# Decoder layer on one core: first norms of blocks 1 to 3 turned before weight and bias, branch products read a row sooner, five value sums on TensorE, projection products placed by load

## The chip, the core and the metric

One core of a Trainium2 chip runs the whole program. The metric is device microseconds of that core. Its engines are TensorE (PE; its weight loads are PEld), VectorE (DVE), ScalarE (ACT), GpSimd (POOL) and SyncE (SP); transfers run on 16 DMA engines. Each engine takes its own instructions in program order and waits on semaphores for the others.

## What is computed

One decoder layer on 512 tokens of width 1024, in f32:

```
z      = x @ W_in                      9 sections of 1024: q, forget, input, out-gate, B, C, h, gate_a, gate_b
o_A    = gated linear recurrence (8 heads) of the first four sections
o_B    = B * causal_depthwise_conv3(C * h)
mix    = (sigmoid(gate_a) * (o_A @ W_a) + sigmoid(gate_b) * (o_B @ W_b)) @ W_out
x      = LayerNorm(alpha * x + mix)
x      = LayerNorm(alpha * x + PEER(x))
x      = x + sigmoid(x @ W_pg) * (p @ W_pp)
```

PEER: queries x @ w_q of 8 heads, two halves each, are scored against 128 keys a half; the 16 best pairs of a head name 16 of 16384 experts. Of each, a row of 2048 numbers (u, then v) is gathered per token, and the output is the sum of softmax weight x gelu(u . x) x v.

## The kernel before

**Rows.** Tokens come in four blocks of 128. A "row" is one of 512 gathers: for 128 tokens, the expert of one head and one rank, 128 x 2048 numbers, 1 MiB. Block b has rows 128b to 128b + 127, 16 for each head. Each engine has a loop over all rows, with fixed work at fixed rows. For row r:

- GpSimd issues the gather into a ring of buffers (`uv`, L726): six, a seventh for rows 98 to 127, more from row 212 on. `row_previous(r)` is the row that had the buffer, `v_reader` the semaphore of the engine that took its v sum; GpSimd waits for that. From row 99 to row 132 it is seven rows back.
- VectorE makes the product u . x (`dot`, L1607).
- ScalarE makes gelu and the coefficient (`row`, L985, L989).
- The v sum, coefficient x v, is taken either by VectorE (rows in `SHARED`; `sum_v` at L1620 into `acc`, one row later) or by TensorE (the others; L2122, two products of 128x512 with a diagonal matrix that ScalarE makes at L997).

In block 0 all rows up to 102 are SHARED, then every third from 109 to 121.

**What else runs under block 0.** The mixer and the first norm of block 0 are done before row 0. For blocks 1 to 3 together (384 tokens) they are spread over the rows of block 0, by tables of rows computed at the top of `build`:

- `UNITS`, rows 0 to 62: 38 of 40 products of 1024 x 128 columns of W_in (h, C, B, then the two gates), eight `unit_mm` each (L2022), in four PSUM banks. The tables name the row `UNIT_ROW` of each product on TensorE; ScalarE (`unit_out`) and VectorE (`conv_in`, `conv_tap`, `conv_out`) read a unit 1 to 4 rows after `UNIT_END`. TensorE doesn't wait for a row as such, only for weights and for the bank's reader four units back. Queries of block 0, heads 4 to 7, stand at rows 0, 4, 14 and 24 (`QUERY0_ROW`).
- `MERGE_ROW`, rows 63 to 86: 16 branch products with W_a and W_b (L2041); VectorE multiplies each with its gate (`merge`, L1373) and adds the two branches (L1378) three rows after its end, the last at row 89.
- `OUT_ROW`, rows 88 to 99: 12 output chunks (L2055), each behind the last merge; VectorE adds the residual three rows later (L1386).
- `NORM_ROW` 95, 99, 103: VectorE's `norm1_stats` (L1393); a row later aggregate and `norm1_scale`: (x - mean) x weight (L1400); two rows later `norm1_shift`: x reciprocal root + bias (L1410), which counts `x1_done`. ScalarE's `root_of` (L978) stands one row after NORM_ROW.
- `TURN_ROW` 98, 102, 106: TensorE transposes the normed block (`turn_x`, L2069), ScalarE copies it out a row later (`turn_out`, L936). SyncE waits for x1_done = 4 before it loads the 4 MiB of `w_gate` (L672) over the place of the first norm's weight and bias; the query weights of heads 2 and on are fetched behind it.
- `QUERY_ROW`, from row 108: queries and scores of blocks 1 to 3; search for the experts of block 1's first heads.

On TensorE, up to row 99 (`JOBS_FIRST`) the tail work of row r comes first and then the v sum of row r - 1; from there the v sum of row r comes first. At row 126 TensorE adds `acc` (`add_acc`), at rows 124 and 129 it makes the second norm's weight and bias rows (`ln2_row`).

## Time and profile before

| | before |
|---|---|
| median of 3 runs | 1788.03 us (1782.82 to 1788.03) |
| profiled execution | 1787.28 us |
| its span, first to last instruction | 1785.3 us |
| busy: PE, DVE, ACT, POOL | 88%, 74%, 44%, 28% |
| gathers | 536.9 of 654.4 MB, 72.9% of the 16 DMA engines' time |
| first gather issued | 336.06 us |

Of the page's 40 slices (44.6 us each) two lines tell most; the first 14 show the mixer of block 0, units and branch products, slices 15 to 19 the stretch of output chunks, norms and first queries and the change from block 0 to block 1:

```profile
DMA  5113289999999999999999999999999999999994
GB/s 210 66 67 141 98 323 397 353 417 409 415 416 416 416 395 356 411 377 413 402 422 410 417 421 422 421 420 422 421 421 422 421 415 422 421 421 419 421 422 180
```

A digit is the busy share in tenths; a rate of about 420 GB/s is what the core reaches in undisturbed slices. In a window's row, the column behind PEclk (granted clock of TensorE as a share of full speed) is the DMA engines' share, then their rate; a share over 1 comes from packets that overlap. In a timeline, idle time before an instruction stands in brackets, with the instruction that ended it. Rows are counted from 0 by L1607's instructions on VectorE (the one at 342.78 us is row 0) and by L726's on GpSimd.

### The profile page before, as it was taken

What the parts mean: (1) busy time and instruction counts of PE and PEld (TensorE: products, weight loads), DVE (VectorE), ACT (ScalarE), POOL (GpSimd) and SP (SyncE); (2) the same over time, 40 slices, a digit from 0 to 9 for tenths busy, and PEclk for the clock granted to TensorE, in tenths of its full rate; (3) what the DMA queues carried; (4) which work ended last, traced back from release to release, by engine and by line L of the source; (5) the groups of instructions that cost most, each with busy time, mean ns of one, the idle gap of its engine ahead of it and who ended that gap; (6) DMA issues with size and microseconds to landing.
All of it is one profiled execution on the core that took longest, in us unless ns stands there. A gap on an engine that the chain in (4) does not pass through costs nothing. (4 is left out here: it accounts for less than half of the span.)

```text
span 1785.3 us, 16920 instructions
## 1 busy us (share of the span) xinstructions
PE 1572.3 (88%) x5008; PEld 876.8 (49%) x5008; DVE 1322.0 (74%) x2717; ACT 780.5 (44%) x1936; POOL 497.0 (28%) x528
## 2 busy tenths in 40 slices
PE   9999999999999978999888668888889879788778
PEld 7888888766555546454344222333333323232224
DVE  4454588699988999578877876876666677766676
ACT  6666695422222124354343434434444443444453
POOL 0000000122332222323333433433333333333341
PEclk9999999999999988999899989999999999999999
DMA  5113289999999999999999999999999999999994
GB/s 210 66 67 141 98 323 397 353 417 409 415 416 416 416 395 356 411 377 413 402 422 410 417 421 422 421 420 422 421 421 422 421 415 422 421 421 419 421 422 180
DMA packets 104501, 654.35 MB, mean 367 GB/s; under 512 B 10336, under 2 KB 25440, under 8 KB 28128
## 3 DMA queue, kind: packets, MB, share of 16 engines
q0 software_dynamic: 73728, 536.90, 72.9%
q1 hardware_dynamic: 30400, 115.92, 17.0%
q8 instruction: 37, 0.61, 0.1%
q10 hardware_dynamic: 288, 0.52, 0.1%
q14 instruction: 48, 0.39, 0.1%
HBM read 651.21 MB, written 2.10 MB: 366 GB/s over the span
## 5 line engine op out<-in xcount | busy, mean ns | idle before, releaser
L2122 PE MATMUL psum<-uv,diag 128*128 128x512 f32 x1400 | 699.8, 631 | 184.2 <-ACT diag L997 180.7
L1607 DVE CUSTOM_DVE_ANT_0 uv<-uv,psum 128x1024 f32<-128x1024 f32 x512 | 623.0, 1217 | 298.3 <-DMA uv<-in_pk_uv,idx 291.8
L726 POOL DMA_INDIRECT uv<-in_pk_uv,idx x512 | 494.6, 966 | 1253.3 <-PE psum L2122 560.3
L2122 PEld LDWEIGHTS psum<-uv,diag 128*128 128x128 f32 x1400 | 254.8, 196 | 600.5 <-ACT diag L997 380.4
L985 ACT ACTIVATE gelu<-dots 128x1 f32<-128x1 f32 x512 | 103.5, 202 | 755.5 <-DVE dots L1607 753.2
L1620 DVE SCALAR_TENSOR_TENSOR oT<-uv,coef,oT 128x1024 f32<-128x1024 f32 x157 | 201.0, 1281 | 1.5 <-ACT coef L989 1.5
L989 ACT ACTIVATE coef<-gelu,weight 128x1 f32<-128x1 f32 x512 | 150.9, 295 | 16.6
L997 ACT ACTIVATE diag<-ident,coef 128x128 f32<-128x128 f32 x350 | 140.6, 402 | 11.5
L2022 PE MATMUL psum<-xT,raw 128*128 128x384 f32 x384 | 125.8, 486 | 0.0
L1858 PE MATMUL psum<-xTh,w_hi 128*128 128x512 f32 x248 | 98.6, 398 | 0.0
L1858 PE MATMUL psum<-xTl,w_hi 128*128 128x512 f32 x248 | 96.8, 390 | 0.0
L1858 PE MATMUL psum<-xTh,w_lo 128*128 128x512 f32 x248 | 96.5, 389 | 0.0
L2022 PEld LDWEIGHTS psum<-xT,raw 128*128 128x128 f32 x384 | 72.4, 190 | 48.8
L2089 PE MATMUL psum<-oT,raw 128*128 128x384 f32 x256 | 92.2, 492 | 0.0
L1133 DVE TENSOR_TENSOR w_lo<-raw_a,w_hi 128x1024 fp32r<-128x1024 f32 x32 | 39.2, 1225 | 69.4 <-ACT w_hi L741 69.1
L2089 PEld LDWEIGHTS psum<-oT,raw 128*128 128x128 f32 x256 | 49.5, 194 | 46.1 <-issue 25.7
L1858 PEld LDWEIGHTS psum<-xTl,w_hi 128*128 128x128 f32 x248 | 46.5, 188 | 10.1
L1858 PEld LDWEIGHTS psum<-xTh,w_lo 128*128 128x128 f32 x248 | 46.6, 188 | 9.1
L1858 PEld LDWEIGHTS psum<-xTh,w_hi 128*128 128x128 f32 x248 | 46.6, 188 | 8.9
L741 ACT ACTIVATE w_hi<-raw_a 128x1024 fp32r<-128x1024 f32 x32 | 34.0, 1062 | 31.4 <-PE psum L1858 27.9
L2185 PE MATMUL psum<-w_gate,x2T 128*128 128x512 f32 x96 | 47.6, 592 | 0.0
L985 ACT ACT_TABLE_LOAD x36 | 46.2, 1283 | 0.6
(295 smaller groups left out, 1856.6 us busy)
## 6 DMA issues: line engine op xcount, KB each, us to landing
raw<-in_w_in SPq DMA_DIRECT2D x24, 1024.0 KB, 8.7
raw_a<-in_w_a SPq DMA_DIRECT2D x12, 1024.0 KB, 4.7
raw<-in_pk_w_q SPq DMA_DIRECT2D x10, 1024.0 KB, 9.1
raw_y<-in_w_in SPq DMA_DIRECT2D x8, 1024.0 KB, 6.8
uv<-in_pk_uv,idx POOLq DMA_INDIRECT x512, 14.7
raw<-in_w_branch_a SPq DMA_DIRECT2D x6, 1024.0 KB, 7.2
raw_w<-in_pk_w_q SPq DMA_DIRECT2D x6, 1024.0 KB, 9.1
raw<-in_w_out SPq DMA_DIRECT2D x5, 1024.0 KB, 14.9
```

Of the source, the lines that this page charges most:

```text
L726: pool.indirect_dma_start(row_uv(r)[:], None, pk_uv, bass.IndirectOffsetOnAxis(idx[:, i % 2, j:j + 1], 0)).then_inc(row_loaded(r)[0], 16)
L985: nc.scalar.activation(gelu[:, r % 4:r % 4 + 1], dots[:, r % 32:r % 32 + 1], ACT.Gelu).then_inc(gelu_done, 1)
L989: nc.scalar.activation(coef[:, r % 8:r % 8 + 1], gelu[:, r % 4:r % 4 + 1], ACT.Copy, scale=weight[:, i % 2, j:j + 1]).then_inc(coef_done, 1)
L997: nc.scalar.activation(diag[:, n % DR, :], ident[:], ACT.Copy, scale=coef[:, r % 8:r % 8 + 1]).then_inc(diag_done, 1)
L1133: V.tensor_tensor(w_lo[:, s], raw_a[:, slot, half], w_hi[:, s].bitcast(F32), ALU.subtract).then_inc(lo_done, 1)
L1607: V.tensor_tensor_reduce(u, u, x_cur[:], 1.0, 0.0, ALU.mult, ALU.add, dots[:, r % 32:r % 32 + 1]).then_inc(dot_done, 1)
L1620: V.scalar_tensor_tensor(out=acc, in0=v, scalar=c, in1=acc, op0=ALU.mult, op1=ALU.add).then_inc(acc_step, 1)
L1858: last = T.matmul(B[bk][:], w[:, s, k, :], xx[:, k, :], start=(k == 0 and i == 0), stop=(k == KT - 1 and i == 2))
L2022: last = T.matmul(B[bank(r)][:, 0:SEQ - P], slot(SLOT["unit", n // 2])[:, k, half * P:half * P + P], xT[:, k, P:], start=(k == 0), stop=(k ...
L2089: last = T.matmul(B[bank(r)][:, 0:n], w[:, k, a * P:a * P + P], turned[:, k, :], start=(k == 0), stop=(k == KT - 1), skip_group_check=True)
L2122: last = T.matmul(B[i][:], diag[:, n % DR, :], row_uv(r)[:, D + i * 512:D + (i + 1) * 512], start=(r in FIRST), stop=last_of_block, skip_g ...
L2185: last = T.matmul(B[6 + i][:], x2T[:, k, :], w_gate[:, k, i * 512:(i + 1) * 512], start=(k == 0), stop=(k == KT - 1), skip_group_check=True)
```

## The change

- Units get their rows from a table of costs (a product 0.654, a query 4.3) so that rows with a query get none or few.
- SHARED leaves out rows 90, 93, 96, 99 and 102: their v sums go to TensorE.
- Merges of the last eight branch products come one row after their end instead of three.
- Norms of blocks 1 to 3: in NORM_ROW statistics and aggregate; the root in the same row; in the next row (x - mean) x reciprocal root (`normed`), which counts x1n_done; TURN_ROW one row earlier. ScalarE puts weight and bias on the transposed copies, eight instructions instead of two per block. The untransposed block gets its weight and bias in rows 109, 113 and 117 (`gained`), which count x1_done. Queries of heads 0 to 2 and what hangs on them come one row earlier.

```diff
--- before.py
+++ after.py
@@ -301,15 +301,27 @@
         X_UNIT = 12
         EARLY = 2
         UNIT_ROW = [[-1] * UNIT_MM] * EARLY
-        UNIT_ROW += [[(UNIT_MM * n + i) * MERGE0 // (UNIT_MM * (len(UNITS) - EARLY)) for i in range(UNIT_MM)]
-                     for n in range(len(UNITS) - EARLY)]
+        UNIT_COST, QUERY_COST = 0.654, 4.3
+        MMS = UNIT_MM * (len(UNITS) - EARLY)
+        ROW_COST = (MMS * UNIT_COST + len(QUERY0_ROW) * QUERY_COST) / MERGE0
+
+        def unit_row(m):
+
+            for r in range(MERGE0):
+                asked = len([q for q in QUERY0_ROW.values() if q <= r])
+                if (m + 1) * UNIT_COST + asked * QUERY_COST <= ROW_COST * (r + 1):
+                    return r
+            return MERGE0 - 1
+
+        UNIT_ROW += [[unit_row(UNIT_MM * n + i) for i in range(UNIT_MM)] for n in range(len(UNITS) - EARLY)]
         UNIT_ROW[EARLY] = [-1] + UNIT_ROW[EARLY][1:]
         UNIT_END = [rows[-1] for rows in UNIT_ROW]
         MERGE_ROW = [MERGE0 + n * 24 // 128 for n in range(16 * KT)]
         OUTS = [(c, b) for b in range(1, TB) for c in range(4)]
         OUT_ROW = [MERGE_ROW[-1] + 2 + n // KT for n in range(len(OUTS) * KT)]
         NORM_ROW = [None] + [OUT_ROW[4 * KT * b - 1] + 4 for b in range(1, TB)]
-        TURN_ROW = [None] + [NORM_ROW[b] + 3 for b in range(1, TB)]
+        TURN_ROW = [None] + [NORM_ROW[b] + 2 for b in range(1, TB)]
+        GAINED_ROW = [None] + [TURN_ROW[-1] + 4 * b for b in range(1, TB)]
         Q0 = TURN_ROW[-1] + 2
         QUERY_ROW = [[Q0 + (n * 5 // 16 if h == 0 else 6 + n * 6 // 16 if h == 1 else 17 + n * 9 // 16)
                       if h < 3 else 123 + 14 * (h - 2) + n * 9 // 16 for n in range(2 * KT)] for h in range(PKH)]
@@ -322,7 +334,7 @@
             b, k = divmod(r, BLOCK_ROWS)
             if b == 0:
                 if r <= OUT_ROW[-1] + 3:
-                    return True
+                    return r < 90 or r % 3 != 0
                 return r % 3 == 1 and 109 <= r <= 121
             if b == 1:
                 return k % 2 == 0 if 4 <= k <= 30 else 30 < k <= 104 and k % 3 == 1
@@ -932,8 +944,11 @@
                 for kh in range(2):
                     r = USE["turn", pc, b, kh]
                     act.wait_ge(t_done, r + 1)
-                    dst = oT[:, 4 * kh:4 * kh + 4, b * P:(b + 1) * P]
-                    nc.scalar.activation(dst, B[bank(r)][:].rearrange("p (k t) -> p k t", t=P), ACT.Copy).then_inc(t_act, 1)
+                    for k in range(4 * kh, 4 * kh + 4):
+                        step = nc.scalar.activation(oT[:, k, b * P:(b + 1) * P], B[bank(r)][:, k % 4 * P:k % 4 * P + P],
+                                                    ACT.Identity, bias=vecs[:, BIAS1 + k:BIAS1 + k + 1],
+                                                    scale=vecs[:, GAIN1 + k:GAIN1 + k + 1])
+                    step.then_inc(t_act, 1)
 
             def query_out(pc, h, parts=range(4)):
                 bs = blocks(pc)
@@ -1007,7 +1022,7 @@
                     if n >= EARLY and r == UNIT_END[n] + (1 if UNITS[n][0] == CHH else 3) and not by_vector_engine(("unit", n)):
                         unit_out(n)
                 for b in range(1, TB):
-                    if r == NORM_ROW[b] + 1:
+                    if r == NORM_ROW[b]:
                         root_of(b, ln_var, ln_root, True)
                     if r == TURN_ROW[b] + 1:
                         turn_out(1, b)
@@ -1416,9 +1431,21 @@
             def norm1_stats(b):
                 dve.wait_ge(*t_reader(USE["out", 1, 3, b]))
                 norm_stats(x_of(b), ln_step)
-
-            def norm1_scale(b):
-                norm_scale(b, tiled(x_of(b)), tiled(x_of(b)), ln1[0], ln_step, ln_var)
+                dve.wait_ge(ln_step, 2 * b + 3)
+                V.bn_aggr(mean_var[:], stats[:].rearrange("p a s -> p (a s)")).then_inc(ln_var, 1)
+
+            def normed(b):
+                norm_rstd(b, ln_root, ln_rec)
+                dve.wait_ge(ln_rec, b + 1)
+                V.tensor_scalar(x_of(b), x_of(b), mean_var[:, 0:1], rstd[:, 1:2],
+                                ALU.subtract, ALU.mult).then_inc(x1n_done, 1)
+
+            def gained(b):
+                x = tiled(x_of(b))
+                dve.wait_ge(t_done, USE["turn", 1, b, 1] + 1)
+                V.tensor_tensor(x, x, ln1[0], ALU.mult).then_inc(ln_step, 1)
+                dve.wait_ge(ln_step, 2 * (TB - 1) + 3 + b)
+                V.tensor_tensor(x, x, ln1[1], ALU.add).then_inc(x1_done, 1)
 
             def stats0(q):
                 dve.wait_ge(*t_reader(USE["out0", q]))
@@ -1443,11 +1470,6 @@
                 V.tensor_tensor(tiled(x0_sb[:]), tiled(x0_sb[:]), ln1[0], ALU.mult).then_inc(ln_step, 1)
                 dve.wait_ge(ln_step, 3)
                 V.tensor_tensor(tiled(x0_sb[:]), tiled(x0_sb[:]), ln1[1], ALU.add).then_inc(x1_done, 1)
-
-            def norm1_shift(b):
-                norm_rstd(b, ln_root, ln_rec)
-                norm_shift(b, tiled(x_of(b)), ln1[1], ln_step, ln_rec, x1_done)
-
 
             LOWEST = float(np.finfo(np.float32).min)
             hot2 = grids[:].rearrange("p s (a b) -> p s a b", b=TOPK)
@@ -1748,7 +1770,7 @@
                     if sect == CB and r == UNIT_END[n] + 2:
                         conv_out(n)
                 for n in range(16):
-                    if r == MERGE_ROW[KT * n + KT - 1] + 3:
+                    if r == MERGE_ROW[KT * n + KT - 1] + (3 if n < 8 else 1):
                         merge(1, n // 4, n % 4)
                 for n, (c, b) in enumerate(OUTS):
                     if r == OUT_ROW[KT * n + KT - 1] + 3:
@@ -1757,9 +1779,9 @@
                     if r == NORM_ROW[b]:
                         norm1_stats(b)
                     if r == NORM_ROW[b] + 1:
-                        norm1_scale(b)
-                    if r == NORM_ROW[b] + 2:
-                        norm1_shift(b)
+                        normed(b)
+                    if r == GAINED_ROW[b]:
+                        gained(b)
 
             for q in range(2):
                 yc_low(q)
@@ -2059,7 +2081,7 @@
 
             def turn_x(pc, b):
                 if b > 0:
-                    pe.wait_ge(x1_done, b + 1)
+                    pe.wait_ge(x1n_done, b + 2)
                 for kh in range(2):
                     if b == 0:
                         pe.wait_ge(x1n_done, kh + 1)
```

## Rows read from the trace of the kernel before

**Rows 1.** Windows: us, busy us (count) of PE, PEld, DVE, ACT, POOL; PEclk, DMA share, GB/s.

```profile
340.00:640.00 300.00, 298.57 (x1065) 185.49 (x1064) 270.60 (x517) 78.14 (x253) 83.72 (x87) 1.00 1.02 414
640.00:720.00 80.00, 60.30 (x239) 45.74 (x238) 78.40 (x144) 26.86 (x68) 22.92 (x24) 0.85 0.96 367
680.00:700.00 20.00, 20.00 (x98) 17.49 (x97) 19.82 (x36) 9.43 (x18) 5.10 (x5) 1.00 0.84 311
720.00:780.00 60.00, 54.17 (x169) 29.23 (x168) 36.64 (x92) 23.17 (x68) 18.82 (x19) 0.94 1.01 419
780.00:820.00 40.00, 37.84 (x124) 20.27 (x123) 32.38 (x71) 20.70 (x53) 13.27 (x13) 1.00 0.94 364
```

**Rows 2.** Waits, 640 to 780 us: who for whom, us in total, times, longest.

```profile
POOL uv L726 <- DVE oT L1620: 60.0, 24, 3.9
```

**Rows 3.** Timeline of VectorE: start us, us, engine line op out<-in xcount [idle before <-releaser].

```profile
342.78 1.22 DVE L1607 CUSTOM_DVE_ANT_0 uv<-uv,psum 128x1024 f32<-128x1024 f32 x1 [0.42 <-ACT psum L973]
...
633.16 1.22 DVE L1607 CUSTOM_DVE_ANT_0 uv<-uv,psum 128x1024 f32<-128x1024 f32 x1 [1.34 <-DMA uv<-in_pk_uv,idx]
...
648.92 1.21 DVE L1607 CUSTOM_DVE_ANT_0 uv<-uv,psum 128x1024 f32<-128x1024 f32 x1
...
655.57 0.54 DVE L1373 SCALAR_TENSOR_TENSOR gbT<-gbT,psum 128x384 f32<-128x384 f32 x1
...
656.62 1.22 DVE L1607 CUSTOM_DVE_ANT_0 uv<-uv,psum 128x1024 f32<-128x1024 f32 x1
...
657.76 1.28 DVE L1620 SCALAR_TENSOR_TENSOR oT<-uv,coef,oT 128x1024 f32<-128x1024 f32 x1
```

**Rows 4.** Timeline of GpSimd: gathers 0, 96, 103, 109 and 133.

```profile
336.06 1.09 POOL L726 DMA_INDIRECT uv<-in_pk_uv,idx  x1 [332.81 <-DVE idx L1572]
...
662.67 0.93 POOL L726 DMA_INDIRECT uv<-in_pk_uv,idx  x1 [2.43 <-DVE oT L1620]
...
684.94 0.94 POOL L726 DMA_INDIRECT uv<-in_pk_uv,idx  x1 [3.50 <-DVE oT L1620]
...
709.27 0.94 POOL L726 DMA_INDIRECT uv<-in_pk_uv,idx  x1 [1.82 <-DVE oT L1620]
...
787.97 0.94 POOL L726 DMA_INDIRECT uv<-in_pk_uv,idx  x1 [6.79 <-PE psum L2122]
```

**Rows 5.** Timeline of TensorE: output chunks, a turn, v sums, query products (two records a product).

```profile
656.80 9.02 PE L2055 MATMUL psum<-raw,gaT 128*128 128x256 f32 x32 [12.71 <-DVE gaT L1378]
...
669.11 10.52 PE L2055 MATMUL psum<-raw,gaT 128*128 128x256 f32 x48
...
696.74 1.04 PE L2069 MATMUL psum<-ident,x_sb 128*128 128x128 f32 x8
...
720.67 3.73 PE L2122 MATMUL psum<-uv,diag 128*128 128x512 f32 x8
724.24 4.68 PE L2089 MATMUL psum<-oT,raw 128*128 128x384 f32 x14
```

**Rows 6.** Line L1436 (first norm of block 0): duration ns min/median/max, first and last start.

```profile
L1436 DVE TENSOR_SCALAR x_sb<-x_sb,mean_var,rstd x2: 540/543/546, 324.6 to 325.0; 128x512 f32<-128x512 f32 x2
```

**Rows 7.** ScalarE: timeline of a root, and line L953, the turned copies of block 0.

```profile
679.62 1.28 ACT L978 ACT_TABLE_LOAD   x1
681.05 0.29 ACT L978 ACTIVATE rstd<-mean_var,eps_ln 128x1 f32<-128x1 f32 x1
...
L953 ACT ACTIVATE ycT<-psum,vecs x8: 448/464/488, 326.6 to 329.0; 128x128 f32<-128x128 f32 x8
```

**Rows 8.** Line L672, the load of w_gate: its issue and its landing.

```profile
L672 SPq DMA_DIRECT2D w_gate<-in_ple_w_gate x1: 327/327/327, 715.5 to 715.5; - x1
...
DMA to landing us min/median/max: 17.9/17.9/17.9
```

**Rows 9.** Block change: row 124's product on VectorE, row 127's v sum on TensorE.

```profile
771.64 1.22 DVE L1607 CUSTOM_DVE_ANT_0 uv<-uv,psum 128x1024 f32<-128x1024 f32 x1
...
785.82 1.88 PE L2122 MATMUL psum<-uv,diag 128*128 128x512 f32 x4
```

## The prediction

> **What bounds the kernel now.** I read the windows first [rows 1]. The kernel gathers 512 rows of 1 MiB, and the core's DMA sets their pace: where nothing disturbs it, it moves 419 GB/s at a share of 1.01 (720 to 780 us), so I take 420 GB/s as full and 1 MiB / 420 GB/s = 2.5 us as one row or one weight chunk. A stretch costs time by what its DMA falls short of that. From 340 to 640 us the share is 1.02 and TensorE is busy for 298.57 of 300 us: no idle DMA to win there. From 640 to 720 the rate is 367 GB/s: (420 - 367)/420 x 80 = **10.1 us** of lost DMA, from 780 to 820 it is 364: **5.3 us**. The change can touch only these.
>
> Next the waits, to see why the DMA starves at 640 to 720. GpSimd issues a gather when the buffer of seven rows earlier (six up to row 97) has been read by the engine that takes that row's v sum. In this stretch it waits for VectorE's sums (oT, L1620) for 60.0 us [rows 2]. VectorE is busy for 78.40 of the 80 us: it bounds there. A row on it is a product (row 90's starts at 656.62, 1.14 us before its sum), a v sum (1.28 us, 1.20 of pitch), search, a merge or residual, and in three rows each statistics, scaling and shift [rows 3]. From gather 96 to gather 109 a row takes (709.27 - 662.67)/13 = 3.6 us instead of 2.5 [rows 4]. TensorE stood for 12.71 us before its first output chunk at 656.80, for the last merged product; then two chunks take 8.9 us, later ones 3.45 each (three in 10.52, 0.17 of it overlap), a turn 1.0 [rows 5].
>
> **The change, part by part.**
>
> *Units by load.* The same products run on TensorE in the same order, the four queries a little earlier among them, their readers one to three rows later, which eats TensorE's lead over the banks. The stretch has no idle DMA: zero, and nothing below it. A stall of TensorE of up to 5 us would be hidden too: it ends the branch products at 656.80 - 12.71 = 644.1, and VectorE wants the last one after 649. I keep +1 as an end.
>
> *Branch products a row behind.* The last two merges (1.05 us each, 655.57 to 656.62 [rows 3]) move from rows 88 and 89 into 86 and 87. Before, row 88 starts at 648.92. Both now come ahead of that, but one more than before also comes ahead of row 83, where VectorE waited 1.34 us for data [rows 3], and so costs nothing. The last merged product is there at 648.92 + 2 x 1.05 - 1.05 = 650.0 instead of 656.7: TensorE starts the output chunks 6.7 us sooner.
>
> *Five v sums to TensorE.* VectorE loses 5 x 1.20 = 6.0 us in rows 91 to 102. But buffers 90, 93, 96, 99 and 102 are now freed by TensorE in its program order: the sum of row 90 stands behind output chunk 3, that of 93 behind chunk 6, that of 96 behind chunk 9 and the first turn, that of 99 behind chunk 11, that of 102 behind the second turn. A sum costs it 1.75 us (two in 3.73, less overlap [rows 5]). From 650.1: 8.9 + 2 x 3.45 + 1.75 = 667.6; + 3 x 3.45 + 1.75 = 679.7; + 3 x 3.45 + 1.0 + 1.75 = 692.8; + 2 x 3.45 + 1.75 = 701.5; + 1.0 + 1.75 = 704.3. They release gathers 96, 100, 103, 106 and 109. Before, 96 went out at 662.67, 103 at 684.94, 109 at 709.27 [rows 4]: **5 and 8 us later than before, and only the last 5 us sooner**. GpSimd takes its gathers in order, so 97 to 99, 101 and 102 wait too, however early VectorE freed theirs.
>
> *What that does to the DMA.* The first gather of all was in use 6.72 us after its issue (336.06 to 342.78 [rows 3, 4]); with 2.5 us of that transfer, a gather starts to move 4.2 us after issue. Gather 95 lands about 665.0 (issued at 658.3); 96 moves from 667.7 + 4.2 = 671.9: 6.9 us idle. 96 to 99 last to 681.9; 100 moves from 684.0: 2.1 us idle. 100 to 102 and a query chunk (fetched when output chunk 8 ends) last to 694.0; 103 moves from 697.1: 3.1 us idle. From there rows 103 to 105, two loads of 1 MiB and rows 106 to 109 keep it full. Sum 12.1 us against 10.1 before: **+2 us**. If chunks 0 and 1 ran at 3.45 us (the pause before them falls from 12.7 to about 6 us, and no row shows L2055 behind such a pause), all from 96 on is 2 us sooner: 0. If each of the first two steps is 1 us slower than counted: +4.
>
> *Norms.* Scale and shift (about the sum's 1.28 us each) become one TENSOR_SCALAR of 1024 columns and, in rows 109, 113 and 117, two TENSOR_TENSOR. The nearest TENSOR_SCALAR takes 543 ns for 512 columns [rows 6]: at most 1.09 us, at least half the sum's 1.28 if its form halves the columns' time; I take 0.9, nearer to that row. VectorE saves some 5 us in rows 96 to 105, and gets 3 x 2.5 = 7.5 us in rows where it waits for data anyway (busy 36.64 of 60 us at 720 to 780 [rows 1]). ScalarE's turn copies become eight: 2.4 us over seven pitches [rows 7], 2.75 us a block. It is busy 9.43 of 20 us at 680 to 700 [rows 1], but its order bites: root 2 now stands behind the first turn's copy, which waits for TensorE until about 691. It comes at 691 + 2.75 + 1.6 = 695 or later, and VectorE stands for some 5 us at row 100. That hides behind the TensorE chain: the gathers it holds (107, 108) stand behind gather 106 anyway.
>
> The Trainium skill's page "ScalarE: Activation LUTs" (section "What ACT_TABLE_LOAD costs") says that a switch of table costs 1.28 us for the load and 1.38 us more to drain. In the trace the root starts 1.43 us after its table load starts (679.62 to 681.05) [rows 7]: the load, and no drain. By the page the stall at row 100 would be 6.4 us instead of 5; either stays behind the TensorE chain, unless that is faster than I count, and then rival 1 pays that 1.4 less.
>
> *The gate weights.* x1_done reaches four at row 117 instead of 105, so SyncE's 4 MiB (issued at 715.5, landed after 17.9 us [rows 8]) move to about 741. The bytes are the same, but they no longer fill the stretch in which TensorE starts the queries. There it needs 16 x 0.65 (seven products in 4.68 us [rows 5]) + 4 x 1.75 = 17.4 us for five rows, 3.5 us a row against 2.5. By my chain the DMA enters it with its queue full to about 720, worth the 5 x 1.0 = 5 us: zero, with an end of +5.
>
> *The block change.* TensorE is full there too: queries, the ln2 rows and the add of the accumulators delay the v sum of row 127 to 785.82 + 1.7 = 787.5, and gather 133 follows at 787.97 after a wait of 6.79 [rows 4, 9]. This paces those rows, and their 5.3 us of idle DMA can swallow the 2 us from ahead. One or two query products more now stand ahead of row 127: up to +1.3. Together -2 to +1.3; I take -1.5.
>
> **Sum.** 0 (units) + 2 (releases) + 0 (norms, gate weights) - 1.5 (swallowed) = +0.5 us. The profiled execution took 1787.28 us (span 1785.3), the median of runs is 1788.03: 1787.28 + 0.5 = **1787.8**.
>
> **Rivals.**
> *1, VectorE's relief pays.* It loses 6 + 5 us of work in rows 90 to 105, as much as the DMA lost. For it: the 60.0 us that GpSimd waits for VectorE [rows 2]. Against it: TensorE's order. If the sums on TensorE come as early as VectorE would give them, idle falls from 10.1 to about 2: -8, 1779.
> *2, slower: releases held by TensorE, and the cover gone.* +2 from the releases, +5 in rows 107 to 111, because the gate weights no longer fill the DMA while TensorE needs 3.5 us a row: +7, 1794. It decides where TensorE comes to the queries later than the DMA's queue lasts, about 720 us. For it: TensorE's steps above; against it: that queue.
> *3, query weights behind the gate weights.* The chunk for h = 2 is fetched right behind the 4 MiB: 741 + 17.9 + 2.5 = 761, wanted at row 124 (its product at 771.64 [rows 9], plus 2). Only if row 117 slips by more than 12 us does TensorE stand; a slip of 15 costs 3: 1791. The skill's page "DMA: Bandwidth & Descriptors" ("Queues, rings and completion order") has one queue's descriptors taken in ring order on each DMA engine, which puts the chunk wholly behind; no row of before has two such loads at this place.
> *4, the change doesn't do what it says.* VectorE takes branch products so early that it waits for TensorE. The margin is 5 us at the last; no change.
>
> **Chances.** Forecast 0.46 (its own range 1785 to 1792: releases 0 to +4, units 0 to +1, block change -2 to +1.3), rival 1 0.27, rival 2 0.18, rival 3 0.04, rival 4 0.05. The range reaches from rival 1's value to just over rival 2's, 1779 to 1795; a time outside has some 0.15. About 0.3% (5.4 us) is what a measurement of this kernel can tell from no change; rivals 3 and 4 are within it. Faster 0.27, same 0.46 + 0.04 + 0.05 = 0.55, slower 0.18.
>
> **What would show it.** TensorE's pause before L2055 falls from 12.7 to about 6 us, from 644 on. GpSimd's waits at 655 to 705 move from L1620 to L2122, with one of about 8 us before gather 96 and two of about 10. The rate at 680 to 700 stays near 311 GB/s or rises little. ScalarE's copies run at 0.34 us of pitch. The gate weights are issued at 735 to 750. I am wrong if gather 96 comes before 664, if the DMA is full from 655 on, or if it shows idle time at 720 to 740.

## The result, and the profile after

| | before | after |
|---|---|---|
| median (range, runs) | 1783.98 us (1782.82 to 1788.03, 6) | 1794.83 us (1792.77 to 1795.27, 6) |
| profiled execution, its span | 1787.28, 1785.3 us | 1794.93, 1792.8 us |

The ratio is 1.0052, with an interval of 1.004 to 1.0064: slower by 9.3 us (7 to 11); the medians lie 10.9 us apart. The forecast of no change (1787.8) was wrong. The time lies in the range, at its upper end, where rival 2 had put it. Between the two profiled executions the difference is 7.65 us, and that is what the two traces have to explain. Lines of the kernel after have moved: L1620 is now L1642, L2122 is L2144, L2055 is L2077, L1607 is L1629, L726 is L738, L2069 is L2091.

First the windows again, with the columns of [rows 1], kernel after:

```profile
640.00:720.00 80.00, 68.51 (x258) 50.11 (x257) 63.87 (x128) 31.55 (x82) 21.12 (x22) 0.94 0.86 338
660.00:680.00 20.00, 19.05 (x77) 15.75 (x78) 14.87 (x31) 6.02 (x15) 3.94 (x4) 0.91 0.50 190
680.00:700.00 20.00, 20.00 (x90) 16.18 (x89) 13.74 (x30) 8.17 (x21) 5.61 (x6) 1.00 0.90 344
720.00:780.00 60.00, 49.42 (x151) 25.57 (x150) 42.35 (x91) 22.66 (x69) 20.30 (x20) 1.00 0.97 390
740.00:760.00 20.00, 18.57 (x60) 10.15 (x59) 13.83 (x41) 6.11 (x20) 6.29 (x6) 1.00 0.90 329
780.00:820.00 40.00, 38.06 (x130) 20.80 (x129) 29.32 (x65) 20.06 (x53) 11.28 (x11) 0.96 0.95 379
820.00:900.00 80.00, 69.76 (x185) 34.13 (x186) 65.79 (x135) 30.14 (x90) 26.76 (x28) 0.96 1.01 419
```

By the prediction's measure, (420 - rate)/420 of a stretch: 640 to 720 us loses 15.6 us (10.1 before), 720 to 780 loses 4.3 (0.1), 780 to 820 loses 3.9 (5.3), and 820 to 900, where the kernel before moved 411 GB/s, loses 0.2 (1.7). Together 24.0 against 17.3, +6.7 of the 7.65 us. The kernel before, profiled a second time (`before again` below, 1781.87 us), loses 8.4, 0.3, 2.2 and 0.2 us in the same four stretches, 11.1 together: the 5.3 at 780 to 820 and the 1.7 at 820 to 900 come and go between executions of one kernel, and nothing is read into changes of that size there. The rises at 640 to 720 and 720 to 780 stand against either profile. So there are two places: **660 to 680 us**, at half the rate, and **740 to 760 us**, where the kernel before was full. VectorE got its relief (63.87 us busy instead of 78.40), and it bought nothing.

The waits say for whom GpSimd stood, 640 to 780 us (engine, line, for whom: us in total, times, longest):

```profile
POOL uv L738 <- PE psum L2144: 74.4, 20, 13.9
POOL uv L738 <- DVE oT L1642: 16.3, 8, 2.5
DVE rstd L1420 <- ACT rstd L993: 7.7, 2, 6.7
DVE best L1492 <- ACT scores L961: 7.5, 2, 6.0
ACT oT L948 <- PE psum L2091: 10.5, 2, 6.7
```

Beside [rows 2]: GpSimd's 60.0 us for VectorE have fallen to 16.3, and it stands 74.4 us for TensorE. Which instructions these were, by the timelines of TensorE and, below the dots, of GpSimd (start us, us; gathers 96, 100, 103, 109 and 133, the same as in [rows 4] with 100 added):

```profile
649.42 8.83 PE L2077 MATMUL psum<-raw,gaT 128*128 128x256 f32 x32 [3.43 <-issue]
660.95 5.41 PE L2077 MATMUL psum<-scores,gaT 128*128 128x256 f32 x16 [2.70 <-DMA scores<-in_w_out]
666.19 3.62 PE L2077 MATMUL psum<-raw,gaT 128*128 128x256 f32 x16
669.64 1.88 PE L2144 MATMUL psum<-uv,diag 128*128 128x512 f32 x4
...
681.72 1.88 PE L2144 MATMUL psum<-uv,diag 128*128 128x512 f32 x4
...
694.67 1.88 PE L2144 MATMUL psum<-uv,diag 128*128 128x512 f32 x4
...
672.30 1.12 POOL L738 DMA_INDIRECT uv<-in_pk_uv,idx  x1 [13.85 <-PE psum L2144]
...
683.87 0.94 POOL L738 DMA_INDIRECT uv<-in_pk_uv,idx  x1 [6.72 <-PE psum L2144]
...
696.83 0.94 POOL L738 DMA_INDIRECT uv<-in_pk_uv,idx  x1 [9.30 <-PE psum L2144]
...
710.11 0.94 POOL L738 DMA_INDIRECT uv<-in_pk_uv,idx  x1 [0.90 <-PE psum L2144]
...
796.19 0.94 POOL L738 DMA_INDIRECT uv<-in_pk_uv,idx  x1 [6.79 <-PE psum L2144]
```

Gather 96 goes out at 672.30, 9.6 us later than before, behind a wait of 13.85 us for the first of the five sums on TensorE; 103 is 11.9 us later, 109 only 0.8, and 133, the first behind the block change, 8.2. The delay seems gone at 109, and gather 128 too is only 1.1 us late (771.35 against 770.27); but by then the kernel before had the 4 MiB of gate weights on the chip (landed at 733.4), while the kernel after lands them at 774.9. At 420 GB/s they are 10 us of transfer, and they fall due at the change of block: from gather 128 to 133 it needs 24.8 us instead of 17.7.

The second place, by the timelines of VectorE and SyncE (the first two lines are the normalize of block 2 with its wait for the root, the third the search in row 115). The two operations of `gained` for row 117 stand at 755.83 and 757.07, and the gate weights go out right behind them, 43 us later than in [rows 8]; the query weights follow them at once:

```profile
701.25 0.16 DVE L1420 RECIPROCAL rstd<-rstd 128x1 f32<-128x1 f32 x1 [6.69 <-ACT rstd L993]
701.45 0.81 DVE L1440 TENSOR_SCALAR x_sb<-x_sb,mean_var,rstd 128x1024 f32<-128x1024 f32 x1
...
747.83 0.49 DVE L1492 MAX8 best<-scores 128x8 f32<-128x128 f32 x2 [6.03 <-ACT scores L961]
...
757.07 1.23 DVE L1448 TENSOR_TENSOR x_sb<-x_sb,gbT 128x1024 f32<-128x1024 f32 x1
...
758.32 0.33 SPq L684 DMA_DIRECT2D w_gate<-in_ple_w_gate  x1
758.69 4.64 SPq L580 DMA_DIRECT2D raw<-in_pk_w_q  x2
```

### The profile page after: what moved, and what is told of

Its sections match the earlier page's. It is cut to its first block and busy times, and to the rows that moved or that the text cites. A ratio compares the mean times of both kernels' runs of the same rounds, so it can differ in the third digit from the quotient of the medians.

```text
span 1792.8 us, 16982 instructions
## 1 busy us (share of the span) xinstructions
PE 1583.1 (88%) x5028; PEld 881.2 (49%) x5028; DVE 1318.1 (74%) x2715; ACT 785.0 (44%) x1958; POOL 501.1 (28%) x528
## 3 DMA queue, kind: packets, MB, share of 16 engines
q1 hardware_dynamic: 30400, 115.92, 16.8%
## 5 line engine op out<-in xcount | busy, mean ns | idle before, releaser
L2144 PE MATMUL psum<-uv,diag 128*128 128x512 f32 x1420 | 709.9, 630 | 188.6 <-ACT diag L1012 185.2
L738 POOL DMA_INDIRECT uv<-in_pk_uv,idx x512 | 498.7, 974 | 1256.6 <-PE psum L2144 596.9
L1629 DVE CUSTOM_DVE_ANT_0 uv<-uv,psum 128x1024 f32<-128x1024 f32 x512 | 623.4, 1218 | 293.1 <-DMA uv<-in_pk_uv,idx 286.1
L2144 PEld LDWEIGHTS psum<-uv,diag 128*128 128x128 f32 x1420 | 258.3, 196 | 608.8 <-ACT diag L1012 392.6
L1642 DVE SCALAR_TENSOR_TENSOR oT<-uv,coef,oT 128x1024 f32<-128x1024 f32 x152 | 194.7, 1281 | 1.5 <-ACT coef L1004 1.5
L1012 ACT ACTIVATE diag<-ident,coef 128x128 f32<-128x128 f32 x355 | 142.6, 402 | 11.6
L1880 PEld LDWEIGHTS psum<-xTl,w_hi 128*128 128x128 f32 x248 | 46.5, 188 | 10.1
L753 ACT ACTIVATE w_hi<-raw_a 128x1024 fp32r<-128x1024 f32 x32 | 34.0, 1061 | 31.6 <-PE psum L1880 27.9
```

What stands on the lines that cost most here:

```text
L738: pool.indirect_dma_start(row_uv(r)[:], None, pk_uv, bass.IndirectOffsetOnAxis(idx[:, i % 2, j:j + 1], 0)).then_inc(row_loaded(r)[0], 16)
L1012: nc.scalar.activation(diag[:, n % DR, :], ident[:], ACT.Copy, scale=coef[:, r % 8:r % 8 + 1]).then_inc(diag_done, 1)
L1629: V.tensor_tensor_reduce(u, u, x_cur[:], 1.0, 0.0, ALU.mult, ALU.add, dots[:, r % 32:r % 32 + 1]).then_inc(dot_done, 1)
L1642: V.scalar_tensor_tensor(out=acc, in0=v, scalar=c, in1=acc, op0=ALU.mult, op1=ALU.add).then_inc(acc_step, 1)
L1880: last = T.matmul(B[bk][:], w[:, s, k, :], xx[:, k, :], start=(k == 0 and i == 0), stop=(k == KT - 1 and i == 2))
L2144: last = T.matmul(B[i][:], diag[:, n % DR, :], row_uv(r)[:, D + i * 512:D + (i + 1) * 512], start=(r in FIRST), stop=last_of_block, skip_g ...
```

## The experiments

All are ratios against the kernel before, run beside it on the same chip; 0.1% is 1.8 us. A cost in us is a difference of medians, which can be a microsecond or two off where the runs scatter; the ratio with its interval stands in the tables. "Lost DMA" is, as above, what a stretch falls short of the full rate, here against 421 GB/s. As a measure it holds for all twenty profiles: their spans run from 1779.2 to 1794.9 us, and the span less the DMA lost at 640 to 900 us is 1767.0 to 1769.0 in every one. The expectations name three theories. R: gathers are held by TensorE's program order. C: the DMA loses its cover, because the gate weights go out late. O: ScalarE's order (root and coefficients behind the turned copies).

| kernel | median us (range, runs) | ratio (interval) |
|---|---|---|
| before again | 1782.58 (1781.59 to 1785.04, 10) | 0.9995 (0.9985 to 1.0005) |
| before + units by load | 1783.81 (1781.53 to 1787.30, 10) | 0.9999 (0.9989 to 1.0009) |
| before + merges a row behind | 1782.07 (1781.11 to 1784.05, 10) | 0.9992 (0.9982 to 1.0001) |
| before + five sums | 1791.34 (1790.66 to 1791.57, 4) | 1.0043 (1.0026 to 1.0059) |
| before + order of norms | 1795.96 (1791.17 to 1797.64, 5) | 1.0058 (1.0039 to 1.0077) |
| after, sums back | 1791.33 (1786.96 to 1794.23, 5) | 1.0045 (1.0031 to 1.0059) |
| after, gain early | 1793.08 (1792.38 to 1793.91, 4) | 1.0054 (1.0038 to 1.0071) |
| after, both | 1788.37 (1787.16 to 1790.65, 8) | 1.0030 (1.0019 to 1.0041) |

**1. The four parts, one at a time.** Each part is laid on the kernel before; the diffs are the ones of the change. The five sums and two undone parts of the kernel after went first:

```diff
 after, sums back
-                    return r < 90 or r % 3 != 0
+                    return True
 after, gain early (rows 107, 109, 111 instead of 109, 113, 117)
-        GAINED_ROW = [None] + [TURN_ROW[-1] + 4 * b for b in range(1, TB)]
+        GAINED_ROW = [None] + [TURN_ROW[-1] + 2 * b for b in range(1, TB)]
```

Sums back:

> The changed kernel with its five v sums (rows 90, 93, 96, 99, 102) back on VectorE. Theory R (releases): the loss is the gathers held behind TensorE's output chunks; the wait of 13.9 us before gather 96 goes, the DMA rate at 660 to 680 us comes back from 190 to over 350 GB/s, and the time falls by 7 to 10 us, to about that of the kernel before. Theory C (cover): the loss is the gate weights that come 43 us later and no longer fill the DMA at 720 to 760, and then starve the gathers at the change of block; the sums matter little: the time falls by at most 3 us.

The five sums alone:

> The kernel before, with only the five v sums moved to TensorE. Theory R: slower than before by 7 to 12 us, since TensorE starts its output chunks 7 us later than in the changed kernel and holds gather 96 until about 678. Theory C: the gate weights still come early (about 715) and cover; no more than 2 us slower, or faster by the 6 us of VectorE's work.

Gain early:

> The changed kernel with weight and bias of the first norms applied in rows 107, 109 and 111 instead of 109, 113 and 117, so that the 4 MiB of gate weights are issued some 20 us earlier. Theory C: idle DMA at 735 to 755 us (329 GB/s at 740 to 760) goes and the gathers of rows 124 to 127 are no longer late: 5 to 9 us less. Theory R: the ring still stalls at 660 to 700; 0 to 3 us less.

Both:

> Both edits: five sums back on VectorE, weight and bias in rows 107, 109 and 111. Theory R: as the run with the sums back, within 3 us. Theory C: as the run with the early weight and bias, within 3 us. If both hold a part, this is the fastest of the four and below the kernel before (by up to 5 us), since the earlier merges and the lighter norms are left with no cost against them.

The five sums alone cost 7.8 us (1791.34 against 1783.56 beside it). GpSimd's longest wait is again the one ahead of gather 96, in that kernel (timeline, then the window 640 to 680 us):

```profile
675.32 1.11 POOL L726 DMA_INDIRECT uv<-in_pk_uv,idx  x1 [15.52 <-PE psum L2122]
...
640.00:680.00 40.00, 29.32 (x113) 22.73 (x112) 33.95 (x69) 6.28 (x24) 9.94 (x11) 0.87 0.70 276
```

(421 - 276)/421 x 40 = 13.8 us of lost DMA stand there, 3.1 in the kernel before. With the sums back in the kernel after, the same stretch moves 406 GB/s (1.4 us lost). R is shown: the five sums hold the gathers, and laid on the kernel before they cost. But in the kernel after, undoing the sums wins only 3.5 us of the 10.9 by the medians and 1.2 by the ratios, an early gain 1.8 and nothing, both 6.5 and 3.9; only the last is clear of the scatter. "Both" is the fastest of the four, as expected if R and C each hold a part, but not below the kernel before. Something else cost more.

Then the rest, with the kernel before itself as a gauge:

> The kernel before, unchanged, profiled beside the next ones, because the runs of before on this kind of chip lie at 1781 to 1786 us while its first profiled execution took 1787.28. Both theories: ratio 1.000 within 0.15%. If the profiled execution is at 1783 to 1784, its idle DMA at 640 to 820 us should be 3 to 4 us less than in the first profile.

> The kernel before with only the last eight branch products read one row after their end. Theory R and theory C alike: the pause of TensorE before the output chunks falls from 12.7 to about 6 us, and since VectorE bounds there the time moves by no more than 2 us (1782 to 1786). Against both: if this alone costs 3 us or more, the loss that is left in the run with the sums back and the early weight and bias (1788.4 against 1783.6) is here.

> The kernel before with only the units placed by load. Both theories: the stretch 340 to 640 us has a full DMA before and after, so nothing moves: 1783.6 within 2 us. If this alone costs 3 us or more, the rest of the loss is here.

> The kernel before with only the new order of the first norms (weight and bias behind the transposes, applied to the rows at 109, 113 and 117; turns and first queries a row sooner); sums on VectorE, merges three rows behind, units as before. Theory C: idle DMA at 720 to 760 us of about 4 us and a late change of block; 4 to 8 us slower than before (1788 to 1791). Theory R: lighter VectorE rows at 96 to 105 and no held gathers: 0 to 4 us faster.

The gauge came out as expected in time (0.9995), and its profile loses 11.6 us at 640 to 900 where the first profile of the same kernel lost 17.9. Units and merges do nothing that can be measured (0.9999 and 0.9992). The merges alone already have a pause of TensorE before output chunk 2 (2.65 us for its weights) and a slow chunk behind it (5.41 us), as the kernel after has, and it costs them nothing. The new order of the norms alone, which the prediction put at 0, is the largest item: 12.4 us by the medians (1795.96 against 1783.58), 10.3 by the ratio, whose interval reaches from 7 to 14. Neither theory had that: C expected 4 to 8 us, R a gain. 12.4 + 7.8 is more than the whole change: both take from 640 to 720 us, where a microsecond can be lost only once, and in the kernel after the earlier merges let gather 96 out 3 us sooner than with the sums alone (672.30 against 675.32).

**2. Three suspects in the norms.** The gate weights alone made late, and the copies alone made eight:

```diff
 before + gate weights late
             sp.wait_ge(x1_done, TB)
+            sp.wait_ge(dot_done, 118)
             sp.dma_start(w_gate
 before + eight copies
-                    dst = oT[:, 4 * kh:4 * kh + 4, b * P:(b + 1) * P]
-                    nc.scalar.activation(dst, B[bank(r)][:].rearrange("p (k t) -> p k t", t=P), ACT.Copy).then_inc(t_act, 1)
+                    for k in range(4 * kh, 4 * kh + 4):
+                        step = nc.scalar.activation(oT[:, k, b * P:(b + 1) * P], B[bank(r)][:, k % 4 * P:k % 4 * P + P], ACT.Copy)
+                    step.then_inc(t_act, 1)
```

> The kernel before with one wait more: the 4 MiB of gate weights also wait for row 117's product, so that they go out at about 750 us instead of 715. Norms, sums, merges, units as before. Theory C (cover): this alone brings back most of what the new order of the norms costs (12 us): idle DMA at 720 to 760 us of 5 us or more, gathers of rows 124 to 127 late, 8 to 13 us slower than before. Theory O (order on ScalarE: roots and coefficients stand behind the turned copies, which wait for TensorE): the gate weights' place is worth little, 0 to 3 us slower.

> The kernel before with the turned copies of blocks 1 to 3 in eight instructions of 128 columns instead of two of 512, without weight and bias, at the same place. Theory O in its weak form (the copies' length, 5 us more in all on ScalarE): 2 to 4 us slower. Theory C, and theory O in its strong form (the place, not the length): within 1 us of before, since the root comes 1.5 us after the copies at 699 and VectorE wants it at 702.

And the kernel after with the sums back, turns and queries a row later, gain in rows 108, 110 and 112, and the root ahead of the turned copies; then the same with gain in rows 105, 107 and 108:

> The changed kernel with the sums back on VectorE, weight and bias in rows 108, 110 and 112, turns and queries at the rows of before, and each root ahead of the turned copy of its row on ScalarE. Theory O: VectorE's wait of about 5 us for a coefficient or root at 695 us goes; deficit of the DMA at 680 to 720 us falls from 9 to under 5; 3 to 5 us less than the run with sums back and early weight and bias (1788.4), so 1783 to 1785. Theory C: the gate weights go out at about 727 as there; within 1.5 us of 1788.4.

> As the run before it, but weight and bias in rows 105, 107 and 108, so that the gate weights go out near 717 as before the change. If C and O hold a part each, this has neither cost and keeps the earlier merges: at or below the kernel before, 1779 to 1783. If it is still 3 us or more above before, a third cost lies in the norms, as VectorE's longer work on them at rows 105 to 108.

Late gate weights (issued at 746.98 instead of 715.5) cost 3.4 us, 1.0019 (1.0009 to 1.0029). The query weights behind them come later too, but TensorE never stands for them; the place of the loss is the change of block, where gathers 128 to 133 take 22.2 us (766.74 to 788.98) against 17.0 in `before again`. In the five kernels whose gate weights go out after 746 us these gathers take 21.8 to 27.9 us, in the other fifteen 17.0 to 20.4. Eight copies cost nothing, 0.9998 (0.9988 to 1.0008): 1784.09 against 1783.95. The root ahead of the copies gave 1788.90, 1.0028 (1.0018 to 1.0038), no better than "after, both" (1.0030), whose turns, queries and gain stand a row sooner, and with an earlier gain 1786.54, 1.0021 (1.0011 to 1.0031). At 640 to 720 us the root-first kernel loses as much DMA as "both", 10.6 and 10.5 us. So theory C was too small, and putting the root first, theory O's cure, did not bring the 3 to 5 us expected of it. The waits of the root-first kernel, 640 to 780 us, and two rows of VectorE's timeline say why:

```profile
DVE oT L1643 <- ACT coef L1004: 10.9, 3, 6.9
...
699.16 1.28 DVE L1643 SCALAR_TENSOR_TENSOR oT<-uv,coef,oT 128x1024 f32<-128x1024 f32 x1 [3.71 <-ACT coef L1004]
...
726.59 1.28 DVE L1643 SCALAR_TENSOR_TENSOR oT<-uv,coef,oT 128x1024 f32<-128x1024 f32 x1 [6.86 <-ACT coef L1004]
```

VectorE no longer stands for the root but for coefficients, which come behind a turned copy just the same: 3.71 us behind that of block 1 and 6.86 us behind that of block 3.

**3. The moves of the norms undone one after another.** What the expectations call "the norms alone" is "before + order of norms" above. Each kernel adds one line to the one ahead of it:

```diff
 (a) gain early
+        GAINED_ROW = [None] + [TURN_ROW[-1] + 2 * b for b in range(1, TB)]
 (b) queries back a row
-        Q0 = TURN_ROW[-1] + 2
+        Q0 = TURN_ROW[-1] + 3
 (c) turns back a row (gain and queries stay at the rows of b)
-        TURN_ROW = [None] + [NORM_ROW[b] + 2 for b in range(1, TB)]
+        TURN_ROW = [None] + [NORM_ROW[b] + 3 for b in range(1, TB)]
 (d) root and normalize back a row
-                    if r == NORM_ROW[b]:
+                    if r == NORM_ROW[b] + 1:
                         root_of(b, ln_var, ln_root, True)
...
-                    if r == NORM_ROW[b] + 1:
+                    if r == NORM_ROW[b] + 2:
                         normed(b)
```

> The kernel before with the new order of the norms alone, and weight and bias of the untransposed blocks in rows 107, 109 and 111 instead of 109, 113 and 117, so that the gate weights go out some 25 us sooner than with the norms alone (756.6 there). The norms alone gave 1.0058. Theory C (late gate weights): their lateness cost 3.4 us in the kernel before, so -3 to -4 here, ratio 1.004. Theory O (what the turn, the root and the queries in sooner rows do to ScalarE and TensorE): about as much as C's share is left, 1.003 to 1.005, with the lost DMA at 680 to 720 us as large as with the norms alone (10.2 us against 6.6 before). If the gate weights interact with the rest, all goes: 1.000 to 1.001.

> As the previous kernel (norms alone, weight and bias at rows 107, 109, 111), with the queries of blocks 1 to 3 and all that hangs on them in the rows they had before, one row later; turns stay a row sooner. If the queries' sooner rows cost (TensorE needs 3.5 us a row there, and the search waited 6.05 us for scores at 746 with the norms alone): 3 us less than the previous kernel, 1.001 to 1.002. If not: within 1.5 us of it.

> As the previous kernel, with the turns of blocks 1 to 3 also back in the rows they had before (98, 102, 106); root and statistics stay a row sooner. Theory O in the turns' form: ScalarE's wait for the turn stands ahead of the coefficients, so a turn after the v sum of its row costs VectorE's waits for coefficients (6.9 us in the norms alone) and they go, -2 to -3 us: 1.000 to 1.001. If the turns' rows do nothing: within 1.5 us of the previous one.

> As the previous kernel, with root and (x - mean) x reciprocal root also back one row: the new arithmetic in the places of the old. What is left against the kernel before is the cheaper arithmetic in rows 97 to 105 and the gate weights about 15 us later. By my theory that the new places, not the new arithmetic, cost: 0.999 to 1.001. If it is still above 1.002, the cost lies in the arithmetic itself, in the late weight and bias (six operations of 1.28 us at rows 107 to 111) or in the gate weights.

| kernel | median us (range, runs) | ratio (interval) |
|---|---|---|
| a | 1790.70 (1789.91 to 1792.26, 5) | 1.0038 (1.0024 to 1.0053) |
| b | 1789.43 (1786.39 to 1793.53, 10) | 1.0028 (1.0018 to 1.0038) |
| c | 1791.62 (1788.52 to 1792.29, 5) | 1.0039 (1.0024 to 1.0053) |
| d | 1786.49 (1783.86 to 1789.73, 10) | 1.0012 (1.0002 to 1.0022) |

Against 1783.83 us beside them that is +6.9, +5.6, +7.8, +2.7 us. Three readings. The early gain brings back 12.4 - 6.9 = 5.5 us by the medians and 3.6 by the ratios (1.0058, 1.0038), whose intervals overlap; the profiles are clearer: lost DMA at 720 to 780 us falls from 7.0 to 0.3 us. That fits the 3.4 us that late gate weights cost in the kernel before. The rows of queries and turns are worth 1.3 and -2.2 us, with intervals that overlap; I read nothing into them, and the expectation that the turns would bring 2 to 3 us failed. The row of **root and normalize** is worth 5.1 us against c (4.8 by the ratios, anything from 2 to 8 by their intervals); against b, which differs in the turns too, d is only 2.9 us faster. So it costs, and how much is known only roughly. The profile has it in two places. One is a wait at 700 us. Kernel c, ScalarE's and VectorE's timelines:

```profile
697.83 2.90 ACT L937 ACTIVATE oT<-psum,vecs 128x128 f32<-128x128 f32 x8 [6.85 <-PE psum L2080]
700.75 1.28 ACT L982 ACT_TABLE_LOAD   x1
702.05 0.29 ACT L982 ACTIVATE rstd<-mean_var,eps_ln 128x1 f32<-128x1 f32 x1
...
702.38 0.16 DVE L1409 RECIPROCAL rstd<-rstd 128x1 f32<-128x1 f32 x1 [5.74 <-ACT rstd L982]
```

Kernel d, the same two:

```profile
695.40 2.90 ACT L937 ACTIVATE oT<-psum,vecs 128x128 f32<-128x128 f32 x8 [6.99 <-PE psum L2080]
698.15 0.24 ACT L989 ACTIVATE gelu<-dots 128x1 f32<-128x1 f32 x1
698.43 0.29 ACT L993 ACTIVATE coef<-gelu,weight 128x1 f32<-128x1 f32 x1
...
698.82 1.28 DVE L1631 SCALAR_TENSOR_TENSOR oT<-uv,coef,oT 128x1024 f32<-128x1024 f32 x1 [3.62 <-ACT coef L993]
```

In both ScalarE stands 7 us for TensorE's turn. In c root 2 comes right behind that copy and VectorE wants it at once: it stands until 702.38, and its next v sum, for which GpSimd waits, behind it. In d a coefficient comes first, VectorE goes on at 698.82, and the root isn't wanted until a row later. The lost DMA at 640 to 720 us is 11.6 us in c and 8.7 in d. The other place is 720 to 740 us, c and then d:

```profile
720.00:740.00 20.00, 18.31 (x50) 9.11 (x50) 16.04 (x22) 8.30 (x28) 7.44 (x7) 0.92 0.90 322
720.00:740.00 20.00, 18.31 (x52) 9.35 (x51) 13.24 (x18) 7.64 (x26) 8.51 (x7) 1.00 0.99 387
```

Behind the stall the rows of c run later, and with them the gain: the gate weights go out at 735.13 in c and at 728.62 in d, and 720 to 780 us loses 4.8 and 2.0. So a part of the difference between c and d reads as late gate weights again; no run separates it from the stall itself.

Summed over 640 to 780 us, VectorE's waits for root and coefficients are 7.4 + 3.9 = 11.3 us in c and 1.5 + 5.3 = 6.8 in d. Kernel a waits 7.1 us, about as long as d, and is 4.2 us slower. It stands for a coefficient behind the turned copy, 4.79 us at 697.70. Its stall goes on to TensorE, which stands for VectorE's residual and then runs a slow chunk (5.38 us instead of 3.45), where d shows a wait of 2.89 and no slow chunk:

```profile
700.13 5.38 PE L2066 MATMUL psum<-raw,gaT 128*128 128x256 f32 x16 [3.42 <-DVE x_sb L1390]
```

That this is the difference between a and d is argued, not shown: no run takes it away alone, and the merges alone have such a chunk at no cost.

**4. Does it hold in the kernel after?** First only three of the five sums go back, then everything that the experiments named:

```diff
 after, two sums (99 and 102) on TensorE
-                    return r < 90 or r % 3 != 0
+                    return r < 99 or r % 3 != 0
 after, places back: sums back, (c) and (d), and
+        GAINED_ROW = [None, 105, 106, 107]
```

> The changed kernel with only the sums of rows 99 and 102 on TensorE; those of 90, 93 and 96 back on VectorE. Gathers 96, 100 and 103 are then released by VectorE, as in the kernel before. Theory R (releases held by TensorE's order): the lost DMA at 640 to 680 us goes (from 11.5 us to 1 to 2), gathers 106 and 109 stay about as late as with five sums, so most of what the kernel with all sums back gained is kept: ratio 1.002 to 1.0045, lost DMA at 680 to 700 about 7. If the mere number of sums on TensorE cost, two fifths of it would be left: 1.005.

> The changed kernel with the sums back on VectorE, root, normalize, turns and queries in the rows of the kernel before, and weight and bias of the untransposed blocks in rows 105, 106 and 107: what is left of the change is units by load, the merges a row behind and the new arithmetic. If the cost of the change is in its places (sums, sooner root, normalize and turn, late gate weights) and not in its arithmetic: 0.9995 to 1.0015, gate weights at about 720 us, VectorE's waits for ScalarE's coefficients under 6 us at 680 to 800. If the arithmetic or the units cost in company: 1.002 to 1.004.

| kernel | median us (range, runs) | ratio (interval) |
|---|---|---|
| after, two sums | 1790.53 (1786.71 to 1794.12, 8) | 1.0038 (1.0026 to 1.0050) |
| after, places back | 1784.95 (1782.64 to 1786.70, 10) | 1.0001 (0.9992 to 1.0011) |

Two sums on TensorE are as good as none (1791.33); it is the early ones, of rows 90, 93 and 96, that hold the gathers. The window 660 to 680 us of the two-sums kernel is full again:

```profile
660.00:680.00 20.00, 17.49 (x80) 15.10 (x81) 19.93 (x41) 5.83 (x15) 6.57 (x7) 1.00 1.00 407
```

Kernel d was just above what was expected of it (1.0012, expected at most 1.001). With the places back in the kernel after and the gain in rows 105 to 107 next to nothing is left (1.2 us by the medians, 0.2 by the ratio), while the new arithmetic, the eight copies, the units and the merges are all still in. Its gate weights go out at 722.65, and 740 to 760 us is at the full rate:

```profile
740.00:760.00 20.00, 20.00 (x65) 11.07 (x65) 16.07 (x46) 7.34 (x23) 6.24 (x7) 1.00 1.01 421
```

So the cost of the change is in three places: the early sums, the sooner root and normalize, and the late gain with the gate weights behind it. That each costs is shown in the kernel before or in the norms alone; what each costs inside the whole change is known only roughly, since they overlap. No kernel here beats the one before by more than the measurement can tell; the nearest is the one with the merges alone.

## Why the prediction was wrong

**The bound and the measure held.** The kernel is slower by what its DMA loses; 640 to 720 us, which was named, lost 5.5 us more, and 720 to 780, which its first paragraph left out of what the change can touch, 4.2 more. VectorE's relief came (-14.5 us busy at 640 to 720), and rival 1, which lets it pay, was wrong for the reason given against it. But it didn't pay with the sums on VectorE either (kernel d 1.0012, places back 1.0001): there VectorE stands 3.6 us for a coefficient behind the turned copy, which waits for TensorE. The forecast was also added to the one profiled execution of 1787.28 us, which lies 3.3 us above the kernel's median of 1783.98: so much of the 1787.8 has nothing to do with the change. None of the prediction's three signs of being wrong came, so they didn't guard the steps that failed.

**Units, merges, copies: right.** 0.9999, 0.9992 and 0.9998. The normalize takes 0.81 us (0.9 taken). TensorE started the output chunks at 649.42 (650.1 predicted), after a pause of 3.4 us instead of the 6 expected; the first two took 8.83.

**Releases: right in mechanism, too small.** +2 us was the term, lost DMA at 640 to 720; the profile shows +5.5 (15.6 against 10.1). The +7.8 of the five sums alone isn't the same term: there, without the earlier merges, TensorE starts its chunks at 656.36, and by the prediction's steps gather 96 would come at 656.36 + 9.56 + 6.9 + 1.75 = 674.6; it came at 675.32. In the kernel after gathers 96, 100 and 103 were put at 5, 7 and 8 us later; it was 9.6, 11.5 and 11.9. The step that failed is the line "8.9 + 2 x 3.45 + 1.75 = 667.6": it lets chunk 2 start right behind chunk 1. It waited 2.70 us for its weights, and then ran 5.41 us instead of 3.45, together 4.7 us, which is the miss of gather 96 (667.7 against 672.30). The prediction didn't use the row of the kernel before that shows it, in the list of DMA issues (KB each, us from issue to landing):

```profile
scores<-in_w_out SPq DMA_DIRECT2D x1, 1024.0 KB, 25.3
```

Issued at 635.70 in the kernel after, with 25.3 us: 661.0, where TensorE starts (660.95). Whoever moves an engine's work forward by 7 us has to look up the landing of each of its operands again. With that, the prediction's own sum of idle DMA (6.9 + 2.1 + 3.1 us) becomes 11.6 + 2.1 + 3.1 = 16.8, and +2 becomes +6.7; the profile's 15.6 is 1.2 us below that. No run fetched these weights sooner with the sums on TensorE, so what the 4.7 us cost in time is read from the trace and not tested.

**Norms at 0, because a VectorE stall "hides behind the TensorE chain": this step failed too.** About 5 us was forecast at row 100 behind root 2; it was 6.69 in the kernel after (701.25). In that kernel it does lie beside gathers held by TensorE. But the norms cost 12.4 us alone, with no sum on TensorE to hide behind. With VectorE's sums back in the kernel after it still stands 4.65 us at the same place (695.01), for a coefficient behind the turned copy instead of the root, GpSimd waits up to 8.3 us for it, and 680 to 700 us moves 276 GB/s. Root and normalize a row later are worth some 3 to 5 us, the gate weights' part in it included. A cover that another part of the same change makes is no cover: where one is wrong, the other is laid bare.

**Gate weights: rival 2 was right, its place wrong.** The zero rested on a DMA queue full to about 720. They went out at 758.32, not 741. The 741 was misread: row 117's product starts at 750.11 in the trace of the kernel before already. In the kernel after it starts at 753.31, behind a search that stood 6.03 us for scores in row 115, and the gain comes behind it. The gap opened at 740 to 760 (329 GB/s) and not in rows 107 to 111, which stand at 718 to 730 us. The price of +5 was near: 4.3 us of lost DMA at 720 to 780, and 3.4 us measured for their lateness alone, 3.6 to 5.5 with the norms.

**Block change: not shown.** The -1.5 rested on 5.3 us of lost DMA at 780 to 820. It is 3.9 in the kernel after, but the kernel before had only 2.2 in its second profile, so that it swallowed anything can't be told from the scatter. Gather 133 came 8.2 us later with the same wait of 6.79 us as before. Rival 3 didn't come, though the gate weights were 17 us later than it took: TensorE has no wait for the query weights at 640 to 860 us.

**The addition.** Forecast: 0 + 2 + 0 - 1.5. Measured: sums 7.8 and norms 12.4 alone, 10.9 all together. Rival 2 needed held releases and a lost cover, and had 0.18; both came, and with root and normalize a third cost that no rival named. That its 1794 meets the measured 1794.83 is in part luck: its +7 stands on the same 1787.28, against a measured difference of 9.3 to 10.9.

## What to carry to other kernels

When a buffer's reader is moved to another engine, its release stands in that engine's program order; write that order down with every wait in it, each operand's landing included, since one late operand moves all releases behind it. Work that is light isn't free if it brings a wait into a row: a root wanted one row after it is asked for, behind a copy that waits for a third engine, cost some 3 to 5 us more here than the same instructions a row later. Before a large load is made later, look at what it filled: one that ran beside a stretch where gathers come too slowly was cover, and its bytes are then moved while the gathers want the DMA (the products of rows 124 to 128 came 6 to 9 us late here).

## What the runs showed of the hardware

An output chunk behind a pause of 2.7 us took 5.41 us, and the granted clock of 660.9 to 666.3 us was 0.68 of full speed, so TensorE ran part of it at the lower of its levels, 1.2 GHz; the next chunk took 3.62 at 1.00. Without a pause, chunks run at 3.45 us, so a wait of 2.7 us held TensorE up by 4.7. The first two chunks took 8.83 us behind a pause of 3.43 and 9.02 behind one of 12.71 [rows 5]: here the work behind a short pause was slowed as much as behind a long one. Two windows of the kernel after:

```profile
660.90:666.30 5.40, 5.35 (x17) 4.45 (x18) 4.92 (x11) 1.29 (x5) 0.00 (x0) 0.68 0.61 255
666.30:669.60 3.30, 3.30 (x17) 2.91 (x16) 1.97 (x5) 0.50 (x2) 0.00 (x0) 1.00 0.04 15
```

In the last one the DMA is all but still: it waits for gather 96.
